# Scaling the differential heads' combined map on GpSimd instead of ScalarE

## The reference

```python
for i in range(S // Q_BLOCK):
    start, end = i * Q_BLOCK, (i + 1) * Q_BLOCK
    p1 = jax.nn.softmax(causal_block_scores(q1[:, :, start:end], k1[:, :, :end], start, scale, slopes), axis=-1)
    p2 = jax.nn.softmax(causal_block_scores(q2[:, :, start:end], k2[:, :, :end], start, scale, slopes), axis=-1)
    a = p1 - lam * p2
    outs.append(jnp.einsum('bhqk,bhkd->bhqd', a.astype(v.dtype), v[:, :, :end]))
```

## Time and profile before

| what | value |
|---|---|
| median of 3 runs | 1302.74 us |
| lowest and highest of them | 1300.78 and 1306.17 us |
| the profiled execution's own time | 1304.77 us |
| its span in the trace | 1302.9 us |
| mean granted TensorE clock | 0.974 of full |
| attention slots of layer 0 | about 90 to 129 us |
| attention slots of layer 1 | about 428 to 467 us |
| experts | about 516 us to the end |

### The profile page before, as it was taken

How to read it: one execution, slowest core, us unless ns; L and a number is a source line. 1 busy time by engine, 2 the same in 40 slices (tenths; PEclk the granted TensorE clock), 3 DMA queues, 4 the chain that set the end, 5 groups by cost and what they waited for, 6 DMA issues and landing times.

```text
span 1302.9 us, 18352 instructions
## 1 busy us (share of the span) xinstructions
PE 1243.3 (95%) x6658; PEld 1052.8 (81%) x6658; DVE 1020.0 (78%) x1107; ACT 822.2 (63%) x862; POOL 144.8 (11%) x139
## 2 busy tenths in 40 slices
PE   6898899999899887999999999999999999999997
PEld 6875799999897676888888888888888888888885
DVE  5886555544568756889989889889889889889886
ACT  5357444444543754777777777677677777777774
POOL 2860000000049102000000000000000000000000
PEclk9888999999899797999999999999999999999999
DMA  9400665555351119999999999999999999999961
GB/s 331 155 15 1 200 201 187 186 176 189 117 178 65 49 46 376 367 369 371 364 366 358 365 359 362 360 369 359 352 374 358 350 377 349 358 372 359 357 238 48
DMA packets 176165, 349.64 MB, mean 268 GB/s; under 512 B 5719, under 2 KB 63637, under 8 KB 176116
## 3 DMA queue, kind: packets, MB, share of 16 engines
q1 hardware_dynamic: 173852, 341.27, 73.9%
q0 software_dynamic: 2064, 7.17, 1.5%
q10 hardware_dynamic: 200, 0.54, 0.1%
HBM read 346.87 MB, written 2.10 MB: 268 GB/s over the span
## 4 chain that ended last, share of the span: by engine, by line
PE 87%; DVE 7%; ACT 3%; issue 2%; DMA 0%; SPq 0%; POOL 0%; POOLq 0%; DVEq 0%; ACTq 0%
PE bank L1482 26%; PE bank L1484 26%; PE bank L1483 26%; PE bank L1797 1%; DVE cv L1127 1%; PE bank L1579 1%; DVE lo_ring L1006 1%; DVE xn L1127 1%; PE bank L1619 1%; ACT hi_ring L690 1%; PE bank L1789 1%; PE bank L1763 1%; PE bank L1778 1%; PE bank L1561 1%; PE bank L1790 1%
## 5 line engine op out<-in xcount | busy, mean ns | idle before, releaser
L1011 DVE TENSOR_TENSOR lo_ring<-raw_m,hi_ring 128x2048 fp32r<-128x2048 f32 x168 | 382.9, 2287 | 53.0 <-ACT hi_ring L696 52.9
L696 ACT ACTIVATE hi_ring<-raw_m 128x2048 fp32r<-128x2048 f32 x168 | 323.0, 1923 | 84.0 <-PE bank L1484 84.0
L1482 PE MATMUL bank<-hi_ring,hT_hi 128*128 128x512 f32 (+2 forms) x896 | 337.2, 376 | 0.0
L1484 PE MATMUL bank<-hi_ring,hT_lo 128*128 128x512 f32 (+2 forms) x896 | 329.5, 368 | 0.0
L1483 PE MATMUL bank<-lo_ring,hT_hi 128*128 128x512 f32 (+2 forms) x896 | 329.1, 367 | 0.0
L1011 DVE TENSOR_TENSOR lo_ring<-raw_a,hi_ring 128x2048 fp32r<-128x2048 f32 x96 | 219.1, 2290 | 32.7 <-ACT hi_ring L696 32.7
L696 ACT ACTIVATE hi_ring<-raw_a 128x2048 fp32r<-128x2048 f32 x96 | 183.4, 1918 | 54.6 <-PE bank L1484 54.6
L1006 DVE TENSOR_TENSOR lo_ring<-raw_a,hi_ring 128x2048 fp32r<-128x2048 f32 (+2 forms) x59 | 132.2, 2244 | 94.8 <-ACT hi_ring L690 94.8
L1482 PEld LDWEIGHTS bank<-hi_ring,hT_hi 128*128 128x128 f32 x896 | 169.6, 189 | 30.3 <-DVE lo_ring L1011 2.4
L1484 PEld LDWEIGHTS bank<-hi_ring,hT_lo 128*128 128x128 f32 x896 | 169.5, 189 | 28.9
L1483 PEld LDWEIGHTS bank<-lo_ring,hT_hi 128*128 128x128 f32 x896 | 169.8, 189 | 27.2 <-issue 0.5
(11 more groups left out here) (277 smaller groups left out, 1409.0 us busy)
## 6 DMA issues: line engine op xcount, KB each, us to landing
raw_m<-in_w_down_exp SPq DMA_DIRECT2D x80, 1024.0 KB, 5.9
raw_a<-in_w_up_exp SPq DMA_DIRECT2D x48, 1024.0 KB, 6.3
raw_m<-in_w_gate_exp SPq DMA_DIRECT2D x48, 1024.0 KB, 6.2
raw_a<-in_w_gate_exp SPq DMA_DIRECT2D x40, 1024.0 KB, 6.2
raw_m<-in_w_up_exp SPq DMA_DIRECT2D x40, 1024.0 KB, 7.2
raw_a<-in_w_in SPq DMA_DIRECT2D x12, 1024.0 KB, 8.0
raw_a<-in_w_gate_dense SPq DMA_DIRECT2D x11, 1024.0 KB, 5.4
raw_a<-in_w_up_dense SPq DMA_DIRECT2D x11, 1024.0 KB, 5.8
```

The lines of the kernel that those rows point to most:

```text
L696: A(hi_of(NA + j), t, ACT.Copy).then_inc(hi_ready, 1)
L1011: V.tensor_tensor(lo_of(NA + j), expert_slot(i, j)[0], hi_of(NA + j).bitcast(F32), ALU.subtract).then_inc(lo_ready, 1)
L1482: M(o, lh, rh, start=start, stop=False)
L1484: return M(o, ll, rh, start=False, stop=stop)
```

## The change

The two multiplications of `scale(k)` leave ScalarE's program. GpSimd does them, one slot after the other, behind its 22 taps. The order on VectorE and TensorE stays as it was, and so do the semaphores: GpSimd waits for `comb_done` and counts `scaled_diff`.

```diff
--- before.py
+++ after.py
@@ -630,6 +630,12 @@
                         pool.wait_ge(tap_done, (POOL_TAPS - 1) * l + w)
                         r = nc.gpsimd.tensor_tensor(cv[:, w % 2, 1, :], tap, cv[:, (w + 1) % 2, 1, :], ALU.add)
                     r.then_inc(pool_taps, 1)
+                for k in range(HEADS):
+                    pool.wait_ge(comb_done, HEADS * l + k + 1)
+                    e = e_sb[:, k % 3, 0, :]
+                    nc.gpsimd.tensor_scalar(e[:, 0:P], e[:, 0:P], coef[:, 2 * k, 0:1], None, ALU.mult)
+                    nc.gpsimd.tensor_scalar(e[:, P:3 * P], e[:, P:3 * P], coef[:, 2 * k, 1:2], None, ALU.mult
+                                            ).then_inc(scaled_diff, 1)
                 if l == LAYERS - 1:
                     pool.wait_ge(mid_mm, MID * l + 4)
                     pool.dma_start(g_bc[:], a["ffn_norm"][l:l + 1, :].broadcast_to([P, D])).then_inc(gfin_in, 16)
@@ -763,12 +769,6 @@
                     if SLOTS * l + k >= 2:
                         act.wait_ge(pv_mm, SLOTS * l + k - 1)
                     A(pt_sb[:, k % 2, :], bank[T_BANK[k % 2]][:, 0:3 * P], ACT.Copy).then_inc(pt_mla, 1)
-
-                def scale(k):
-                    act.wait_ge(comb_done, HEADS * l + k + 1)
-                    u, e = units_of(k)[0], e_sb[:, k % 3, 0, :]
-                    A(e[:, 0:P], e[:, 0:P], ACT.Copy, scale=coef[:, u, 0:1])
-                    A(e[:, P:3 * P], e[:, P:3 * P], ACT.Copy, scale=coef[:, u, 1:2]).then_inc(scaled_diff, 1)
 
                 for p in range(NIN):
                     act.wait_ge(piece_used, in_done(l, p))
@@ -847,7 +847,6 @@
                                       bank[MID_BANK[10 + r3]][0:NOPE, :].rearrange("p (h t) -> p h t", h=2), ACT.Copy))
                     if p == 7:
                         exponentials(0)
-                scale(0)
                 for k in range(SLOTS + 3):
                     if 1 <= k < SLOTS:
                         exponentials(k)
@@ -876,8 +875,6 @@
                         A(hT_hi[:, 2 + 5 - j, :], bank[O_BANK[j % 2]][:, 0:T], ACT.Copy).then_inc(cat_hi["mla"], 1)
                     if HEADS <= k - 2 < SLOTS:
                         copy_transposed(k - 2)
-                    if 2 <= k <= HEADS:
-                        scale(k - 1)
 
                     if k == 13:
                         mid(15)
```

## The result

Six executions of the changed kernel took 1310.02 us in the median (1306.52 to 1311.61), six of the kernel before on the same chip 1303.17 (1299.0 to 1306.17). The ratio is **1.005**, with an interval from 1.0031 to 1.007: 6.5 us slower, on the edge of the 0.5% within which the prediction called it the same, and inside its range. The profiled execution took 1310.71 us with a span of 1308.9, which is 6.0 more than the span of before.

The account below looks back on a forecast made before the run. TensorE, busy 95%, was taken to hold the chain, which in slot 4 runs through the scaling. Later scaled maps cost 2.2 us per layer, +4.4 in all, from median 1302.74 to 1307.1, stated as 1307.0; range 1302 to 1313.

Parts of the forecast that it names:

- The lateness: Slots 0 to 5: GpSimd's hand-over and two instructions take 1.59 us against 0.83, so each scaled map comes 0.76 us later.
- The cheap pair: Rival: GpSimd's two scaling instructions with hand-over take 0.91 us, 0.1 us later than now; +0.2 us, 1303; chance 0.15.
- the dear one: Rival: both GpSimd scaling instructions take 0.94 us or more, 1.1 us late; +7.0 us, 1309.7; chance 0.15.
- Slots 1, 2 and 4: Transposes get later by 0.4, 0.4 and 0.8 us per layer; 0.4 us of slack in the first two, none in slot 4.
- the 0.62: Slots 1 and 2: us from scaled map to transposes; 0.2 booked for weight load and hand-over, leaving 0.4 slack.
- Slot 3: Its transposes start some 3 us behind the scaling, so the later scaled map costs 0.
- Slot 0: Transposes hidden with 0.6 us to spare, but VectorE is held up 0.5 us, some 0.3 of it slack; 0.2 booked.
- is held until 92.2: Slot 0: VectorE's L1134 at 91.70, reading two SBUF tensors, must wait for GpSimd's scaling to end; 0.5 us.
- Slot 5: Scaled at 113.45, transposes at 113.89 behind the values; 0.4 us of slack, so 0.4 us later.
- The sum: Slots 0, 1, 2, 4 and 5 lose 2.2 us per layer, nothing behind takes it up; +4.4 us for both layers.
- the clock comes back later: Rival: waits before 108 us delay the rise to full clock, 3.5 us per layer; +11 in all, 1314; chance 0.1.
- ScalarE's relief: ScalarE gets back 4.8 us per layer, booked at nothing; as a rival, at most 3.2 us gained, 1299.7, chance 0.04.

Follow-up runs that it names:

- e3: Kernel before with two throwaway copies ahead of the scaling on ScalarE, GpSimd not used; 1305.44 us, ratio 1.0015.
- e5: Kernel before with GpSimd scaling slots 0 and 3 only, ScalarE the other four; 1303.89 us, ratio 1.0005.
- e6: Kernel before with GpSimd scaling the narrow 128 columns as soon as they are combined, ScalarE the wide 256; 1303.7 us, ratio 1.0001.
- e8: Changed kernel with throwaway matmuls filling TensorE's waits in slots 4 and 5; 1306.34 us, ratio 1.0024 to the kernel before.
- e4: Kernel before with GpSimd scaling slots 1, 2, 4 and 5 only, ScalarE slots 0 and 3; 1309.08 us, ratio 1.0053.
- e9: The changed kernel measured once more, with a second profile; 1309.08 us, ratio 1.0035 to the kernel before.
- e1: The kernel before, unchanged, measured against itself; 1302.93 us, ratio 1.0001.
- e2: Kernel before with the scaling left out, transposes waiting for the combine; 1302.5 us, ratio 0.9994.
- e7: Kernel before with ScalarE scaling both pieces, the narrow one as soon as its half is combined; 1303.51 us, ratio 0.9992.
- e11: Changed kernel with throwaway matmuls in all its slots, seven ahead of slot 4's transposes; 1304.37 us, ratio 1.0007 to the kernel before.
- e12: Kernel before with throwaway matmuls in its slots, none ahead of slot 3's transposes, and ScalarE's narrow scaling started early; 1296.21 us, ratio 0.995.
- e10: Kernel before with throwaway matmuls in all its slots, 28 per layer; 1298.39 us, ratio 0.9961.

## Why the prediction was right, and where not

**The lateness (0.76, used as 0.8): right.** Measured 0.77. The wide piece took 0.92 (0.94 booked), the narrow one 0.605 (0.56), the hand-over 0.10 (0.09); the records of the two pieces overlap by 0.02. The cheap pair is out and so is the dear one. The rule of the Trainium skill, "GPSIMD Engine Reference", section "4.1 Engine selection", that one-input operations are roughly line-rate, does not hold for this form: 0.92 us beside ScalarE's 0.49 for the same 256 columns, and VectorE's multiplication of 256 columns by a tap (L1123, the form of L629) took 0.35 in the kernel before.

**Slots 1, 2 and 4 (0.4, 0.4, 0.8): right.** Measured 0.47, 0.46 and 0.78. The slack is 0.30 and not 0.4, found with GpSimd and with ScalarE (e3); the 0.2 that I took off the 0.62 for weight load and hand-over was in no row, and comes out as 0.32. The wait in slot 4 was to grow from 1.03 to about 1.8; it is 1.77.

**Slot 3 (0): right,** by the steps and by e5, which holds slot 0 too.

**Slot 0 (0.2): wrong.** The step that failed is that VectorE's sum of the taps "is held until 92.2". It should have taken about 0.9 us. L1131, which is L1134 of before, took 0.42 as before, starting at 91.95 while GpSimd's wide piece ran from 91.37 to 92.29. Both its inputs are in SBUF. So it was not held. The narrow piece alone was slower beside VectorE's tap, 0.77 for 0.60, as it was in e6. The first transposes came 0.13 earlier, not later. The kernel before could have warned me. There a multiplication of GpSimd (L629) that started ahead of VectorE's split was the one that waited, while the split took its usual time:

```profile
42.91 3.10 POOL L629 TENSOR_SCALAR xn<-u_pad,dw 128x256 f32<-128x256 f32 x1
...
43.02 2.28 DVE L1006 TENSOR_TENSOR lo_ring<-raw_a,hi_ring 128x2048 fp32r<-128x2048 f32 x1
```

I had read one case in which GpSimd came second as if the engine that starts first always went first. The Trainium skill, "SBUF — State Buffer", section "SBUF: two separate sides", has the shared ports as a lock that such a VectorE sum takes too and that the first to start keeps. Neither L1131 at 91.95 nor L629 at 42.91 agrees.

**Slot 5 (0.4): size right, reason only in part.** The step is 0.53 longer in layer 0, but with the clock down, and the chain goes by L1257 and the values. With the clock held (e8) it is 3.91 against 3.49: 0.42, released by GpSimd, as booked.

**The sum (+4.4): right as the part that is lateness.** Slots 1, 2, 4 and 5, with the clock held behind slot 4, make 0.47 + 0.46 + 0.78 + 0.42 = 2.13 per layer, 4.3 in all (2.2 and 4.4 booked). That it is so near is partly luck: the 0.2 of slot 0 did not come, and slots 1 and 2 cost 0.13 more than booked. From slot 0's transposes to the first output projection the time grew by 3.06 us in layer 0 and 2.27 in layer 1, where I had said 2.2 for each.

**The term that is missing.** Two measurements of the change gave 1.0050 and 1.0035, the middle of which is 5.5 us, and e4 1.0053. With the clock held behind slot 4 it was 1.0024, 3.1 us (e8). About 2.4 us thus seem to come with the clock. Each of these numbers has an interval of 1.7 us or more to either side, so this one is rough, and e3, whose clock fell behind slot 4 as well, shows no such cost. I had a rival on the clock, but for the wrong place: "the clock comes back later" out of the stretch from 92 us. It did not. The clock fell *again*, behind the wait in slot 4, and against that I had argued that pauses "do not cost the clock once it is there". That sentence failed. The stretch that it rested on holds a pause of 1.87 us at full clock, longer than the 1.77 that the change made:

```profile
122.25 0.49 PE L1640 MATMUL bank<-xn,v_m 128*128 128x128 f32 x2 [1.87 <-ACT xn L765]
```

So one pause that cost nothing is no evidence for the next. Counted over the profiles: where slot 4 waits 1.54 us or more on an otherwise idle TensorE (after, e9, e4, e3), a new low stretch begins within 3 us behind the transposes in both layers, eight of eight times. Where it waits at most 1.03 (before, e1, e2, e5, e6, e7) it does so in none of six in layer 0 and in two of six in layer 1 (e1, e7). With the wait filled (e8) in neither layer. That the longer wait brings the clock down behind slot 4 is shown by e8 and by this count; what that costs is known only roughly. The length of the wait is not all, though. The pause of 1.87 us at 122.25 stands in every kernel and both layers (at most 0.01 us apart), and within 3 us behind it the clock fell in 11 of 28 cases: in after, e8 and e9 in one layer each, in e2, e4, e11 and e12 in both, in before, e1, e3, e5, e6, e7 and e10 in neither.

The low stretches further on are thus not settled. After, e9 and e4 each have one that begins between 123 and 130 and one between 160 and 164, but e2 has them at 120 and 154, e1 and e7 one at 157 to 158, e10 one at 157 and e12 at 118 and 155, with no GpSimd in the slots.

**Where the 6.0 us of the two spans lie.** From start to slot 0's transposes -0.1; slots 0 to 5 +2.25; on to the output projection (128.59 and 131.52) +0.8; to the norm +0.7; layer 1's way to its slots +1.1; its slots +0.7, as the clock was back earlier there; on to its output projection +1.6; behind that -1.0. This is bookkeeping on one execution of each, and the single entries carry the chance in the clock.

**ScalarE's relief (booked at nothing): right.** Its busy time fell by 7.8 us. In e2, where nobody is late for it, the steps into slots 1, 2 and 5 did not shorten, and the whole of what e2 took away is worth at most 1.8 us.

## What to carry to other kernels

Moving a small operation to an idle engine pays only if the whole way from producer to consumer gets shorter: compare hand-over plus durations on both engines, slot by slot, with the slack that the timeline shows, not the busy shares. A slack found while TensorE runs at 1.2 GHz is gone once that is mended (0.3 us in slots 1 and 2). And where the granted clock is 0.50, cheap matmuls that fill TensorE's waits can be worth more than a move of work like this one: 28 per layer gave 5.1 us here, and 24 with the narrow piece scaled early 6.5 us, each against the kernel before.

## What the runs showed of the hardware

- GpSimd's multiplication by a per-partition scalar takes 0.605 us for 128 and 0.924 us for 256 columns, so 2.5 ns per column and 0.29 us fixed; with an addition in the same instruction it was 0.55 us for 256. One more operand made it faster, and no run says why.
- A VectorE sum of two SBUF tensors (0.42 us) ran unhindered beside GpSimd's wide multiplication, while GpSimd's narrow one went from 0.60 to 0.77 us beside VectorE's multiply-and-add, and a wide one (L629, 42.91 us) from 0.93 to 3.10 beside VectorE's split, which began after it.
- TensorE was busy for all of 92 to 108 us and yet granted 0.50. Its work there is scores with 32 rows, values, transposes and, ahead of slot 3, sums of 128 x 256 (L1693). With matmuls of 128 x 128 put between (e10), the same stretch ran at 1.00, and ended sooner with more work in it. The low stretch began at 91.0, in a wait of 1.87 us, which eight of the matmuls fill; why the clock then stayed down over 17 us of work, and which of the matmuls held it up, no run tells.
- Over executions of the kernel before, the total follows the mean granted clock, about 1.4 us for each 0.001 (1305.7 us at 0.974, 1301.4 at 0.977). Between programs it does not: e2 ran at 0.970 to 0.974 in 1302.5 us.
